# The scores of a head's two attention maps in the two row halves of the PE array

## What is computed

```python
def diff_attn_block(q, k, v, q_pos, k_pos, lam):
    s = jnp.einsum('bqhmd,bkhmd->bhmqk', q, k).astype(F32) * (HEAD_DIM ** -0.5)
    mask = (k_pos[None, :] // CHUNK) <= (q_pos[:, None] // CHUNK)
    s = jnp.where(mask, s, -jnp.inf)
    p = jax.nn.softmax(s, axis=-1)
    p = p[:, :, 0] - lam * p[:, :, 1]
    return jnp.einsum('bhqk,bkhe->bqhe', p.astype(v.dtype), v)
```

## Time and profile before

| | us |
|---|---|
| runs, median of three (lowest to highest) | 2641.35 (2639.3 to 2654.49) |
| the profiled execution | 2640.45 |
| its span, first to last instruction | 2638.1 |
| PE busy | 2034.5 (77%) |
| DVE busy | 1589.0 (60%) |
| ACT busy | 697.5 (26%) |
| mean granted PE clock | 0.914 |

### The profile page before, as it was taken

How to read it: one execution, slowest core, us unless ns; L and a number is a source line. 1 busy time by engine, 2 the same in 40 slices (tenths; PEclk the granted TensorE clock), 3 DMA queues, 4 the chain that set the end, 5 groups by cost and what they waited for, 6 DMA issues and landing times.

```text
span 2638.1 us, 37877 instructions
## 1 busy us (share of the span) xinstructions
PE 2034.5 (77%) x11684; PEld 1183.5 (45%) x11684; DVE 1589.0 (60%) x4244; ACT 697.5 (26%) x1690; POOL 793.1 (30%) x831
## 2 busy tenths in 40 slices
PE   6999898888777666665779999988886776656565
PEld 4566687664343312211255667866652442211112
DVE  2544216666766788787634342365657678887875
ACT  2422213332222222222224222133313132222223
POOL 0022103233444344444201220023334433444441
PEclk9999999999898888788889999989998988888888
DMA  7134558999999999999752346499999999999996
GB/s 207 29 99 146 182 191 349 417 418 408 417 419 405 418 413 412 410 406 416 325 150 59 91 145 209 161 392 417 410 418 420 419 401 415 421 417 413 413 414 250
DMA packets 206463, 852.42 MB, mean 323 GB/s; under 512 B 19824, under 2 KB 91008, under 8 KB 124352
## 3 DMA queue, kind: packets, MB, share of 16 engines
q0 software_dynamic: 95280, 677.21, 62.4%
q1 hardware_dynamic: 110992, 172.89, 18.8%
HBM read 843.33 MB, written 6.71 MB: 322 GB/s over the span
## 4 chain that ended last, share of the span: by engine, by line
PE 24%; DMA 24%; issue 15%; DVE 12%; PEld 12%; PEldq 5%; DVEq 3%; ACT 2%; POOL 2%; ACTq 0%; POOLq 0%; SPq 0%
PE ps L727 9%; DMA MIX_RINGS<-in_peer_uv_dram,IDX 9%; DMA W<-in_peer_uv_dram,IDX 8%; DMA WQKV_E<-in_peer_uv_dram,IDX 6%; PEld ps L791 5%; PEldq L952 4%; PE ps L967 4%; PEld ps L950 3%; PE ps L739 3%; DVEq L1363 2%; DVE MIX_RINGS L1515 2%; PEld ps L856 2%; DVE W L1515 1%; PE ps L755 1%; PE ps L773 1%
## 5 line engine op out<-in xcount | busy, mean ns | idle before, releaser
L950 PE MATMUL ps<-MIX_RINGS,GC 64*64 64x512 f32 x3712 | 636.7, 690 | 207.7 <-ACT GC L1169 160.8
L675 POOL DMA_INDIRECT MIX_RINGS<-in_peer_uv_dram,IDX x400 | 441.0, 1103 | 791.1 <-PEq L952 444.9
L950 PE MATMUL ps<-W,GC 64*64 64x512 f32 x1840 | 384.7, 713 | 237.4 <-ACT GC L1169 216.3
L950 PEld LDWEIGHTS ps<-MIX_RINGS,GC 64*64 64x64 f32 x3712 | 181.3, 152 | 521.1 <-issue 521.1
L675 POOL DMA_INDIRECT W<-in_peer_uv_dram,IDX x182 | 201.0, 1105 | 435.6 <-PEq L952 359.7
L1169 ACT ACTIVATE GC<-twins,WV 128x64 f32<-128x64 f32 x640 | 170.4, 336 | 569.0 <-DVEq L1528 566.5
L1515 DVE CUSTOM_DVE_ANT_0 MIX_RINGS<-MIX_RINGS 128x1024 f32<-128x1024 f32 x224 | 268.4, 1223 | 77.6 <-DMA MIX_RINGS<-in_peer_uv_dram,IDX 69.6
L1515 DVE CUSTOM_DVE_ANT_0 MIX_RINGS<-MIX_RINGS,WQKV_E 128x1024 f32<-128x1024 f32 x176 | 213.0, 1224 | 158.6 <-DMA MIX_RINGS<-in_peer_uv_dram,IDX 151.7
L950 PEld LDWEIGHTS ps<-W,GC 64*64 64x64 f32 x1840 | 105.3, 154 | 441.3 <-issue 441.3
L727 PE MATMUL ps<-WQKV_E,HT 128*128 128x384 f32 x768 | 252.8, 486 | 0.7 <-issue 0.7
L1163 ACT ACTIVATE GV<-AV 128x4 f32<-128x4 f32 x160 | 32.9, 205 | 717.6 <-DVEq L1516 717.4
(11 more groups left out here) (257 smaller groups left out, 2741.5 us busy)
## 6 DMA issues: line engine op xcount, KB each, us to landing
W<-in_merge_w_dram SPq DMA_DIRECT2D x40, 1024.0 KB, 4.9
W<-in_merge_w_dram SPq DMA_DIRECT2D x60, 512.0 KB, 14.1
WQKV_E<-in_w_in_dram SPq DMA_DIRECT2D x48, 512.0 KB, 6.6
W<-in_query_w_dram SPq DMA_DIRECT2D x16, 1024.0 KB, 11.6
W<-in_w_in_dram SPq DMA_DIRECT2D x12, 1024.0 KB, 9.6
W<-in_query_w_dram SPq DMA_DIRECT2D x20, 512.0 KB, 9.4
W<-in_out_w_dram SPq DMA_DIRECT2D x8, 1024.0 KB, 14.4
MIX_RINGS<-in_peer_uv_dram,IDX POOLq DMA_INDIRECT x400, 13.4
```

The costliest lines, as they stand in the source:

```text
L675: pool.indirect_dma_start(UV[r], None, table, bass.IndirectOffsetOnAxis(IDX[:, n % 2, j:j + 1], 0))\
L950: pe.matmul(ps[o:o + CHUNK, n:n + 512], w[r, :], v[r, d * 512:(d + 1) * 512], start=False, stop=False, skip_group_check=True)
```

## The change

QT has one plane instead of two: 128 partitions, map 0 in the first 64, map 1 in the others, without zeros. ACT fills it in one copy of 128 partitions, and qt_ev counts one a head. A score matmul reads the 64 partitions of its map of QT and KT, and each map has a bank of its own: (3, 7) for tile 0, (4, 6) for tile 1, (5, 2) for tile 2. The signal s_ps now comes from a drain after each tile's two matmuls. Since bank 7 takes scores too, the wait for o_ev, which stood before the value products, stands before the scores, with a nop behind it. DVE masks and reduces the maps of tiles 0 and 1 one by one.

```diff
-        QT = cut(2, TOKD, at=0)
+        QT = cut(TOKD, at=0)
...
+        def scores(t, m):
+            return bank(((3, 7), (4, 6), (5, 2))[t][m], 0, (P, 2 * P, PAST + DEC_SEQ)[t])
...
-                pe.wait_ge(*qt_ev.at(l, h * 2 + 2))
+                pe.wait_ge(*qt_ev.at(l, h + 1))
                 pe.wait_ge(*kt_ev.at(l, h + 1))
                 pe.wait_ge(*ptb_ev.at(l, h))
+                d = [slice(m * HD, (m + 1) * HD) for m in range(2)]
+                pe.wait_ge(*o_ev.at(l, h))
+                pe.nop(nofuse=True)
                 for t in range(2):
                     n = (t + 1) * P
                     for m in range(2):
-                        out = bank(4 if t == 0 else 6, m * n, (m + 1) * n)
-                        i = pe.matmul(out, QT[:, m, t * P:(t + 1) * P], KT[:, 0:n], start=True, stop=True)
-                    i.then_inc(s_ps.sem, 1)
+                        pe.matmul(scores(t, m), QT[d[m], t * P:(t + 1) * P], KT[d[m], 0:n],
+                                  start=True, stop=True)
+                    pe.drain().then_inc(s_ps.sem, 1)
                 for m in range(2):
-                    i = pe.matmul(bank(5 if m == 0 else 2, 0, PAST + DEC_SEQ), QT[:, m, 2 * P:3 * P],
-                                  KT[:, SEQ:SEQ + PAST + DEC_SEQ], start=True, stop=True)
-                i.then_inc(s_ps.sem, 1)
+                    pe.matmul(scores(2, m), QT[d[m], 2 * P:3 * P],
+                              KT[d[m], SEQ:SEQ + PAST + DEC_SEQ], start=True, stop=True)
+                pe.drain().then_inc(s_ps.sem, 1)
...
-                pe.wait_ge(*o_ev.at(l, h))
                 pe.wait_ge(*pta_ev.at(l, h + 1))
...
-                for m in range(2):
-                    d = slice(m * HD, (m + 1) * HD)
-                    act.activation(QT[d, m, :], bank(2, 0, TOKD)[d], ACT.Copy).then_inc(qt_ev.sem, 1)
+                act.activation(QT, bank(2, 0, TOKD), ACT.Copy).then_inc(qt_ev.sem, 1)
...
-                        maps = bank(4 if t == 0 else 6, 0, 2 * n).rearrange("p (m k) -> p m k", m=2)
-                        dve.memset(maps[0:CHUNK, :, n - CHUNK:n], FAR)
+                        for m in range(2):
+                            dve.memset(scores(t, m)[0:CHUNK, n - CHUNK:n], FAR)
                         fence()
-                        dve.tensor_reduce(mxs[:, t, :], maps, AX_X, ALU.max)
+                        for m in range(2):
+                            dve.tensor_reduce(mxs[:, t, m:m + 1], scores(t, m), AX_X, ALU.max)
...
-                dve.memset(QT[HD:P, 0, :], 0.0)
-                dve.memset(QT[0:HD, 1, :], 0.0)
```

More of the change, by code:

```diff
@@ L354, in build @@
         qt_ps = signal("qt_ps", HEADS)
-        qt_ev = signal("qt_ev", 2 * HEADS)
+        qt_ev = signal("qt_ev", HEADS)
         kt_ps = signal("kt_ps", HEADS)
@@ L1144, in head @@
                     for m in range(2):
-                        src = (bank(4, m * n, (m + 1) * n), bank(6, m * n, (m + 1) * n),
-                               bank(5 if m == 0 else 2, 0, n))[t]
+                        src = scores(t, m)
                         act.activation(PR[t][:, m, :], src, ACT.Exp, bias=nb[:, t, m:m + 1], scale=SCALE,
```

## The result

| | before | after |
|---|---|---|
| median, us | 2641.4 (2639.3 to 2654.49, 20 runs) | 2647.16 (2644.67 to 2654.27, 20 runs) |
| ratio to before, 95% interval | | 1.0018 (1.0010 to 1.0026) |
| span of the profiled execution | 2638.1 | 2644.7 |
| attention, layer 0 and layer 1 | 179.0, 178.9 | 182.0, 181.8 |

The change costs 0.18%, 4.8 us by the ratio. That is within the 1% to which the chances were given and inside the range, but its sign is clear, and the prediction had -1.7 us. Attention is counted here from head 0's first transpose of Q to the first transpose behind the merge products (L1025 before, L1033 after). It grew by 3.0 and 2.9 us, 5.9 of the 6.6 us between the spans.

What follows compares the result with a forecast made beforehand. PE was taken to set attention's pace. Fourteen middle heads at -0.18 us (-2.5) and two last heads (+0.8) gave -1.7 us, so 2639.5 us, range 2632 to 2656.

Steps and rivals of the forecast that it cites:

- Term 1: Score matmuls on PE: two maps run fully at once, leaving 1.20 us and saving 1.19 us a head.
- The quadrants: Experts' 64*64 matmuls, taken as nearest to the new scores: sixteen passes in 2.00 us, so four run at a time.
- one after the other: Rival in the scores: the maps don't overlap, term 1 is lost, +16.7 us, 2656 us; chance 0.06.
- half of it: Rival in the scores: program-order starts let only one pass overlap, three passes a pair, +8.4 us, 2648 us; chance 0.05.
- terms 2 and 3: PE around a head's scores: three drains, 0.92 us, and the switch from 128 to 64 rows, 0.09 us.
- term 2: Drains behind a head's three score tiles on PE cost 0.26, 0.26 and 0.40, in sum 0.92 us a head.
- The clock rival: Granted clock falls to 1.2 GHz in the projection after the scores: 2.6 us a head, +36, 2676 us; chance 0.03.
- Covers: Middle heads: DVE's extra 0.25 to 0.45 us lies under 6.0 us of idling; Q copy and moved wait are hidden too.

Runs made afterwards that it cites:

- one signal a tile: The changed kernel without drains, s_ps raised once a tile by the second map's matmul alone; 0.9968 (0.9956 to 0.9980) of the time before.
- DVE's part alone: The kernel before with only a memset and a reduction for each map of tiles 0 and 1 instead of one for both; 1.0001 (0.9992 to 1.0010).

## Why the prediction was wrong

**Term 1 was right.** Two maps at once save what was reckoned. The change against the kernel before with drains: (166.08 - 159.13)/7 = 0.99 us a head; 1.19 less the switch (0.09) and its stretched pass (0.10) is 1.00. The quadrants were the right row to go by, and "one after the other" and "half of it" fell: the two maps' passes lie side by side.

**The failed step is the sum of terms 2 and 3 for a middle head: it prices a drain and the switch by their gaps alone.** The gaps were read rightly: the single passes of the changed kernel leave 0.25, 0.25 and 0.38 us behind the tiles and 0.09 ahead of them, where 0.26, 0.26, 0.40 and 0.09 stood in the sum. But each was counted as the idle time up to the next start, and what the gap does to the matmul behind it was left out: 0.10 us more in its first pass, four times a head. 2.21 + 4 x 0.10 = 2.61 against 2.39 is +0.22; measured +0.20. The row was there: in the earlier trace rows the eight passes of L866 behind a drain take 1.15 us, while eight in a row take 7 x 0.11 + 0.27 = 1.04. I read its start and not its length. In the kernel before, three drains cost 1.18 us a head where term 2 had 0.92. Over 14 heads this is 5.3 of the 7.6 us between the forecast and the change in the trace (-1.7 and +5.9).

**The last head.** The forecast was +0.4 us a layer from the sequencer's wait, the nop and DVE. At full clock it is nothing (13.35 us in the head without the fall). The scores started 2.75 us after the first Q transpose before and after, so the wait and the nop cost nothing; DVE's split cost 0.15, not 0.35, and the earlier first tile (DVE starts 0.60 us after the first score, before 0.78) made that up.

**The clock rival was right in kind and wrong in place.** It was priced for the middle heads, with 0.03. There the long projections stood on both sides and the clock stayed at 1.00. Against it I set that idle times of 1.66 and 1.14 us had left the clock up. That was true of all six last heads before; at the same 1.66 us it fell in five heads of six after. At 1.5 to 1.7 us a head it is 3.2 us of the profiled execution. Why the change brings it on stays open. Without it the change would still have cost 2.8 us by the trace, and the forecast had a gain.

**A number that fits by chance.** The rival "half of it" had 2648 us, 1 us from the median measured. Its mechanism didn't occur: the two maps ran fully side by side, and the time came from the stretched passes and the clock.

**Covers.** DVE's added instructions, ACT's single Q copy and the moved wait were free in middle heads, as argued.

## What to carry to other kernels

A drain between short matmuls costs its gap and also the weight load that nothing hides any more: read the length of the first pass behind a gap, not only when it starts. If the only purpose of the drain is a signal, let the matmuls raise it themselves; here that turned +0.18% into -0.34%. And where PE must wait for another engine, even 1.66 us can be followed by half the clock for up to 6.8; half of a product that is due anyway kept the clock up through such a hole, though here it fell at PE's next wait instead.

## What the runs showed of the hardware

- A switch from 128 to 64 rows costs 0.09 us and 0.10 us more in the first pass; the way back without a drain the same (the projection began 0.09 us after the scores' array time in the kernel without drains).
- The stretched pass is 0.10 us whatever its columns (128, 256, 320 or 384). The Trainium skill (TensorE: Matmul & The Clock Gate, LDWEIGHTS) gives a weight load's time by its columns alone, divided by 1.2, in ns; for 128 columns that comes to an estimate of 107 ns, and the trace agrees with its 0.10 of stretch. The rows of the loads themselves last longer, 0.18 to 0.19 us.
- The clock's fall doesn't need a fully idle PE for long: 1.66 us of waiting were followed by 0.50 within 0.5 us of the first score in five of six last heads after, in both with drains in the kernel before, in one of two with one signal a tile, and in none of the ten others with this wait (six before, two without drains, two with DVE's part alone). With the wait filled it was none of six. In four of these eight falls the clock went down ahead of the first score pass or with it. Why some heads escape stays open.
